# The head, the pair boundaries and the last norm of a two-block transformer kernel, put in another order

## The reference, cut to what matters

```python
def adaln(cond, w_ada, b_ada):                       # w_ada: 1024 x 3072
    m = jax.nn.silu(cond) @ w_ada + b_ada
    return jnp.split(m, 3, axis=-1)                  # shift, scale, gate

def hybrid_layer(...):
    shift, scale, gate = adaln(c, w_ada, b_ada)
    shift_c, scale_c, gate_c = adaln(c_ctx, w_ada, b_ada)
    h = rmsnorm(x, norm_g) * (1 + scale[:, None]) + shift[:, None]       # 1024 tokens
    hc = rmsnorm(ctx, norm_g) * (1 + scale_c) + shift_c                  # 256 tokens
    q, k, v, za, u, bg, cg, zc = jnp.split(h @ w_in, SPLIT_POINTS, axis=-1)
    q, k = rmsnorm(heads(q), q_norm_g), rmsnorm(heads(k), k_norm_g)
    kc, vc = jnp.split(hc @ w_in[:, D_ATTN:3 * D_ATTN], 2, axis=-1)
    attn = neighbourhood_attention(q, k, heads(v), kc, vc, rpb) * silu(za)
    conv = bg * centred_short_conv(cg * u, conv_w, conv_b) * silu(zc)
    x_new = x + gate[:, None] * (concat([attn, conv]) @ w_out)
...
    return _rmsnorm(x, g_final)                      # the end of the second block
```

## Time and profile before

| | us |
|---|---|
| three runs, median | 2747.57 |
| the three runs | 2745.29, 2747.57, 2747.58 |
| the profiled execution's own time | 2748.74 |
| its span | 2746.9 |
| PE busy | 2587.7 |
| DVE, ACT, POOL busy | 1107.1, 803.1, 765.7 |

### The profile page before, as it was taken

The page is one execution under the profiler, slowest core; times in us unless marked ns, Lnnn a source line. Parts: engine busy times, 40 slices in busy tenths (PEclk is TensorE's granted clock), DMA queues, the critical chain, the costliest instruction groups (busy, mean ns, idle before and its releaser), DMA issues.

```text
span 2746.9 us, 34507 instructions
## 1 busy us (share of the span) xinstructions
PE 2587.7 (94%) x12792; PEld 2128.9 (78%) x12792; DVE 1107.1 (40%) x1758; ACT 803.1 (29%) x1326; POOL 765.7 (28%) x492
## 2 busy tenths in 40 slices
PE   7899999999899999999999899997999999999997
PEld 2677877888787878778787688885788888888886
DVE  3553555545545544445444553444242121121123
ACT  3343444434412443344433521232021010010110
POOL 1131314122247222222222133323233333333331
PEclk9899999999999999999999999998999999999998
DMA  8412213030345222211222134210211111111111
GB/s 310 145 57 78 64 48 99 19 115 31 132 131 171 71 71 67 70 60 61 70 66 70 69 122 168 92 47 31 77 61 48 51 46 47 52 46 46 53 46 69
DMA packets 68165, 218.25 MB, mean 79 GB/s; under 512 B 21180, under 2 KB 21436, under 8 KB 63172
## 3 DMA queue, kind: packets, MB, share of 16 engines
q1 hardware_dynamic: 45316, 123.67, 14.2%
q10 hardware_dynamic: 22720, 92.81, 10.3%
HBM read 173.43 MB, written 35.16 MB: 76 GB/s over the span
## 4 chain that ended last, share of the span: by engine, by line
PE 74%; issue 7%; DVE 6%; ACT 5%; DMA 4%; POOL 1%; SPq 1%; ACTq 0%; DVEq 0%; POOLq 0%
PE ps L1869 14%; PE ps L1870 13%; PE ps L1872 13%; PE ps L1856 8%; PE ps L1857 8%; PE ps L1858 8%; DMA raw<-in_w_stream_dram 2%; PE ps L2262 1%; DMA ada<-in_w_ada_dram 1%; PE ps L2090 1%; PE ps L2066 1%; DVE stage L1679 1%; SPq L380 1%; ACT pt_hi L671 1%; ACT p_hi L968 1%
## 5 line engine op out<-in xcount | busy, mean ns | idle before, releaser
L410 POOL CAST w_hi<-raw 128x1024 fp32r<-128x1024 f32 x192 | 208.3, 1085 | 1753.1 <-issue 783.6
L1856 PE MATMUL ps<-act_hi,w_hi 128*128 128x512 f32 x1168 | 471.5, 404 | 12.3 <-POOL w_lo L412 9.0
L412 POOL TENSOR_TENSOR w_lo<-raw,w_hi 128x1024 fp32r<-128x1024 f32 x192 | 470.8, 2452 | 15.4
L1857 PE MATMUL ps<-act_lo,w_hi 128*128 128x512 f32 x1168 | 461.1, 395 | 5.6 <-issue 5.6
L1858 PE MATMUL ps<-act_hi,w_lo 128*128 128x512 f32 x1168 | 461.5, 395 | 0.0
L1869 PE MATMUL ps<-act_hi,w_hi 128*128 128x512 f32 x1008 | 396.4, 393 | 9.9 <-DVE act_lo L1208 5.3
L1870 PE MATMUL ps<-act_lo,w_hi 128*128 128x512 f32 x1008 | 394.8, 392 | 0.0
L1872 PE MATMUL ps<-act_hi,w_lo 128*128 128x512 f32 x1008 | 312.2, 391 | 0.0
L1856 PEld LDWEIGHTS ps<-act_hi,w_hi 128*128 128x128 f32 x1168 | 222.5, 190 | 53.2 <-POOL w_lo L412 9.2
L1858 PEld LDWEIGHTS ps<-act_hi,w_lo 128*128 128x128 f32 x1168 | 222.3, 190 | 49.3
L1857 PEld LDWEIGHTS ps<-act_lo,w_hi 128*128 128x128 f32 x1168 | 223.1, 191 | 45.5 <-issue 6.5
(11 more groups left out here) (360 smaller groups left out, 3926.2 us busy)
## 6 DMA issues: line engine op xcount, KB each, us to landing
raw<-in_w_stream_dram SPq DMA_DIRECT2D x192, 512.0 KB, 3.5
ada<-in_w_ada_dram SPq DMA_DIRECT2D x6, 2048.0 KB, 9.7
spill<-res ACTq DMA_DIRECT2D x16, 512.0 KB, 5.1
gate_dram<-gate_sb ACTq DMA_DIRECT2D x32, 256.0 KB, 2.0
stage<-spill ACTq DMA_DIRECT2D x16, 512.0 KB, 4.0
res<-in_x_t_dram ACTq DMA_DIRECT2D x1, 4096.0 KB, 19.3
rope_sb<-in_rope_dram ACTq DMA_DIRECT2D x4, 1024.0 KB, 4.9
stage<-in_x_t_dram ACTq DMA_DIRECT2D x8, 512.0 KB, 4.4
```

Source lines behind the costliest of these rows:

```text
L410: nc.gpsimd.tensor_copy(w_hi[:, s, :, :], raw[:, s, :, :]).then_inc(S["w_hi"], 1)
L412: nc.gpsimd.tensor_tensor(w_lo[:, s, :, :], raw[:, s, :, :], w_hi[:, s, :, :].bitcast(F), ALU.subtract).then_inc(S["w_split"], 1)
L1856: nc.tensor.matmul(out, wh, xh, start=start, stop=False)
L1857: nc.tensor.matmul(out, wh, xl, start=False, stop=False)
```

## The change

**Head.** The two halves of x are loaded first of all on ACT's queue. W_ada gets three buffers at the start; SP then loads block 3, tiles 0 and 1, ctx, blocks 4 and 5, tiles 2 and 3, and only then issues the Toeplitz transfers and the strip. In blocks 0 to 3 two of eight slices stay in plain fp32; the other six are split on the chip: ACT copies to fp32r (`ada_hi`, three copies of 128x1024 a block), DVE subtracts (`ada_lo`), and PE makes twelve fp32r matmuls with four columns of cond (high and low), whose rows are added after the transposes. Tiles 0 and 1 are projected together, slice by slice. The gate blocks come behind them as `gate_chunk`: W_ada is the stationary operand and one column of cond moves, so 32 products a block. The norm of ctx lies between and behind them, then the ctx keys.

**Pairs.** First half of Q's tile, ctx keys and second half of Q's tile move ahead of the pair's start, to the end of the pair before; the `hc` load moves to unit 14. Between `head_ss` and first spread stands the first half of V; the second half of V comes before `half_turn` of K, and only the ctx values are left between that and the second spread. Tile 4 is done in two halves, with the scores of units 0 and 1 and, behind the second, three convolution steps; ACT evacuates u after the first exponential. In the last pair convolution steps are kept for units 14 and 15, its mix is split in another order, and the first two W_out tiles take slices 0 to 3 before 4 to 7.

**End.** The last output tile is made in token halves, and square, sum, spread, scale and store follow half by half.

```diff
-                             w_stream[s].rearrange("p (k c) -> p k c", k=KT)
-                             ).then_inc(S[f"raw_in{s}"], 16)
+            def ada_load(n, used=0):
+                if used:
+                    sp.wait_ge(S["ada_used"], used)
+                sp.dma_start(ADA_SLOT[n], w_ada[n].rearrange("p (k c) -> p k c", k=KT)).then_inc(S[ADA_IN[n][0]], 16)
+
+            def tile_load(idx):
+                if idx >= 2:
+                    sp.wait_ge(S["w_split"], idx - 1)
+                sp.dma_start(raw[:, idx % 2, :, :], w_stream[idx].rearrange("p (k c) -> p k c", k=KT)
+                             ).then_inc(S[f"raw_in{idx % 2}"], 16)
+
+            ada_load(0)
+            ada_load(1)
+            ada_load(2)
+            ada_load(3, 1)
+            tile_load(0)
+            tile_load(1)
+            sp.dma_start(ctxF[:, :, :], ctx_t).then_inc(S["rows_in"], 16)
+            ada_load(4, 2)
+            ada_load(5, 3)
+            tile_load(2)
+            tile_load(3)
 
...
@@ -389,10 +410,12 @@
                                  w_stream[bass.ds(2 * h + s, 1)].rearrange("o p (k c) -> (o p) k c", k=KT)
                                  ).then_inc(S[f"raw_in{s}"], 16)
 
-            for k in range(KT):
...
@@ -421,7 +444,6 @@
             split(0, 0, free=False)
             split(0, 1, free=False)
 
-            pool.wait_ge(S["mask_in"], 16)
...
+                nc.scalar.activation(csq[:, k % 2, :], ctxF[:, k, :], ACT.Square).then_inc(S["sq_ready"], 1)
+
+            ada_hi(0)
+            for k in range(4):
+                x0_square(k)
+            ada_hi(1)
+            for k in range(4, 8):
+                x0_square(k)
+            ada_row(0)
+            ada_hi(2)
+            ada_row(1)
+            norm_rms("x0")
+            ada_hi(3)
+            ada_row(2)
+            ada_row(3)
             nc.scalar.activation(turn[:, :, :], traw[:, :].rearrange("p (a m) -> p a m", a=2), ACT.Copy)
-
-            act.wait_ge(S["ada_used"], 4)
-            nc.scalar.activation(mrow[:, 0:2 * D], ps[0:2, 0:4 * BANK], ACT.Copy).then_inc(S["ada_rows"], 1)
-            norm_rms("x0")
+            norm_hi("x0", {6: [lambda: ctx_square(0)], 7: [lambda: ctx_square(1)]})
+            for k in range(2, KT):
...
@@ -660,6 +712,8 @@
                     nc.scalar.activation(osh[here, :], na_o(m)[there, :], ACT.Copy).then_inc(S["na_osh"], 1)
 
                 exp_unit(0)
+                act.wait_ge(S["tile_done"], t0 + 5)
+                nc.scalar.activation(cv_x, ps[:, 4 * BANK:6 * BANK], ACT.Copy).then_inc(S["cv_u"], 1)
                 for u in range(16):
                     if u < 15:
                         exp_unit(u + 1)
@@ -673,7 +727,12 @@
                                          ).then_inc(S["na_pt_hi"], 1)
                     if u >= 2 and u % 2 == 0:
                         other_half(u // 2 - 1)
-                    for h in HALF_TAKEN.get(u, []):
+                    if u == 14 and not last_pair:
+                        act.wait_ge(S["na_scores"], 16 * i + 16)
+                        act.wait_ge(S["hc_saved"], 32)
+                        act.dma_start(hc_hi[:, :, :].bitcast(F), hc_dram[:, 0, :, :]).then_inc(S["hc_in"], 16)
+                        act.dma_start(hc_lo[:, :, :].bitcast(F), hc_dram[:, 1, :, :]).then_inc(S["hc_in"], 16)
...
+                if last_pair:
+                    act.wait_ge(S["tile_done"], T_OUT)
+                    mixed_hi(0)
...
+                    dve.wait_ge(S["hi_ready"], 4 * n + j + 1)
+                    nc.vector.tensor_tensor(act_lo[:, 3 * (n % 2) + j, :],
+                                            ADA_SLOT[n][:, 2 * j + 2:2 * j + 4, :].rearrange("p k c -> p (k c)"),
+                                            act_hi[:, 3 * (n % 2) + j, :].bitcast(F), ALU.subtract
+                                            ).then_inc(S["lo_ready"], 1 if j < 2 else 2)
+
+            ada_lo(0)
+            for k in range(4):
+                accumulate("x0", k, stage[:, k % 2, :])
+            ada_lo(1)
...
-            pe.wait_ge(S["c_silu"], 1)
-
             def ada_chunk(n):
-                pe.wait_ge(S[f"ada_in{n % 2}"], 16 * (n // 2) + 16)
-                for k in range(KT):
-                    last = nc.tensor.matmul(ps[0:2, (n % 4) * BANK:(n % 4 + 1) * BANK], cond[:, k, :],
-                                            ada[:, n % 2, k, :], start=(k == 0), stop=(k == KT - 1))
+
+                out = ps[0:4, n * BANK:(n + 1) * BANK]
+                pe.wait_ge(S[ADA_IN[n][0]], ADA_IN[n][1])
+                for k in range(2):
+                    nc.tensor.matmul(out, cond4[:, k, :], ADA_SLOT[n][:, k, :], start=(k == 0), stop=False)
+                for j in range(3):
+                    pe.wait_ge(S["lo_ready"], 4 * n + j + 1)
+                    for k in range(2):
+                        x = slice(k * BANK, (k + 1) * BANK)
+                        for part in (act_hi, act_lo):
+                            last = nc.tensor.matmul(out, cond4r[:, 2 * j + 2 + k, :], part[:, 3 * (n % 2) + j, x],
+                                                    start=False, stop=(j == 2 and k == 1 and part is act_lo))
                 last.then_inc(S["ada_used"], 1)
 
-            def turn_rows(m0, m1, b):
-
-                for m in range(m0, m1):
-                    last = nc.tensor.transpose(bank(b, 2 * m, 2 * m + 2), mrow[:, m * P:(m + 1) * P], ident[0:2, 0:2])
-                last.then_inc(S["ada_turned"], 1)
-
+            def gate_chunk(n):
+
+                pe.wait_ge(S[ADA_IN[n][0]], ADA_IN[n][1])
+                for m in range(4):
+                    for k in range(KT):
+                        c = 64 + 4 * (n - 4) + m
+                        last = nc.tensor.matmul(bank(4, c, c + 1), ADA_SLOT[n][:, k, m * P:(m + 1) * P],
+                                                cond4[:, k, 0:1], start=(k == 0), stop=(k == KT - 1))
+                return last
+
+            pe.wait_ge(S["c_sig"], 4)
             for n in range(4):
+                if n == 3:
+                    sum_squares("x0")
                 ada_chunk(n)
-            sum_squares("x0")
-            pe.wait_ge(S["ada_rows"], 1)
-            turn_rows(0, 16, 4)
+            spread("x0")
+            pe.wait_ge(S["ada_rows"], 4)
+            for m in range(16):
+                last = nc.tensor.transpose(bank(4, 4 * m, 4 * m + 4), mrow[:, m * P:(m + 1) * P], ident[0:4, 0:4])
+            last.then_inc(S["ada_turned"], 1)
+
+            tile_ready(T_ATT)
+            tile_ready(T_ATT + 1)
+            for k in range(KT):
+                for s in range(2):
+                    last = project(s, 2 * s, act_hi, act_lo, T, [k], filled("x0") if s == 0 else None, k == 0,
+                                   k == KT - 1)
+                    if k == KT - 1 and s == 0:
+                        last.then_inc(S["half_done"], 2)
+            gate_chunk(4)
             sum_squares("ctx")
-            spread("x0")
+            gate_chunk(5).then_inc(S["ada_turned"], 1)
             spread("ctx")
-            ada_chunk(4)
-            ada_chunk(5)
-            pe.wait_ge(S["ada_rows"], 2)
-            turn_rows(16, 24, 2)
-
-            tile_ready(T_ATT)
-            project(0, 0, act_hi, act_lo, T, ready=filled("x0")).then_inc(S["half_done"], 2)
+
+            def context_keys(i):
+                pe.wait_ge(S["hc_in"], 32 * i + 32)
+                return project(0, 6, hc_hi, hc_lo, C, ready=filled("ctx"))
+
+            context_keys(0).then_inc(S["tile_done"], 2)
+            pe.wait_ge(S["ada_step"], 5)
 
             def neighbourhood(i, last_pair):
...
@@ -1975,15 +2166,15 @@
                     last.then_inc(S["qk_perm"], 1)
 
                 head_ss(0, tD, 0)
-                project_half(1, 2, 1).then_inc(S["tile_done"], 1)
+                tile_ready(t0 + 2)
+                pe.wait_ge(S["pair_done"], i + 1)
+                project_half(0, 4, 0)
                 pe.wait_ge(S["ck_rms"], 2 * i + 1)
                 nc.tensor.matmul(bank(6, C, 2 * C), bd64, ksq, start=True, stop=True).then_inc(S["ck_ss"], 1)
                 head_spread(0, tD, 0)
-                tile_ready(t0 + 2)
-                project_half(0, 4, 0)
                 head_ss(1, tB, 2)
+                project_half(0, 4, 1)
                 half_turn(0, kh, 0)
-                project_half(0, 4, 1)
                 pe.wait_ge(S["conv_done"], i + 1)
...
@@ -2052,7 +2243,9 @@
 
                 scores(0)
                 scores(1)
-                done = 0
+                project_half(0, 4, 1).then_inc(S["tile_done"], 1)
+                conv_steps(0, 3)
+                done = 3
...
                         if u == 14:
@@ -2091,11 +2284,18 @@
                                                         start=(n == 0 and pt is pt_hi),
                                                         stop=(n == len(blocks) - 1 and pt is pt_lo))
                         last.then_inc(S["na_pv"], 1)
+                if not last_pair:
```

(28 more changed lines are left out.)

348 lines of the change are left out of this document (237 added, 111 removed).

## The result

The changed kernel took 2772.83 us, median of four runs (2770.34 to 2775.81), beside 2746.43 for the kernel before on the same chip: a ratio of 1.0096, 95% interval [1.0083, 1.011]. That is 26.4 us slower, where the forecast had 9.6 and a range that ended at 2770. The profiled execution spans 2770.6 us against 2746.9, so 23.7 us are there to be found in the trace.

The account below looks back on a forecast made before the run. PE's work plus its idle time was taken as the bound; +22.1 + 7.6 + 4.6 - 13.4 - 4.0 - 7.3 = +9.6 us on the profiled 2748.74 is 2758.3, forecast 2757 because that execution lies 1.2 above the median; range 2740 to 2770.

Parts of the forecast that it names:

- The sign: Whole kernel: the change makes it slower, +9.6 us in sum.
- the head: Start to second spread of pair 0: uncovered gate blocks and ctx behind x move that spread from 134.05 to 156.2, +22.1 us.
- The row at 52.12: Earlier profile's stretch granted 0.50 after PE's one- and two-column matmuls; taken as evidence that gate blocks fall to low clock.
- Last pair and W_out: Last pair's end: six steps for units 14 and 15 shrink waits, six thinner units open 0.3 each; -4.0 us.
- clock and exponential terms: Per pair: low clock behind the wait at the second spread costs 1.9 us, the earlier first exponential saves 3.35.
- Boundaries: Between pairs, last P times V to second spread: 42.4 us at jumps, 40.8 without; +1.8 plus issue stalls, +4.6 us.
- the stall: 2.8 us issue stall behind each of two jumps: full price or hidden in a wait, so half taken twice, +2.8 us.
- Low clock: Second spread, four times: PE waits 6.0 us for DVE, then runs at low clock, 1.9 us each, +7.6 us.
- First exponential: Start of units, four pairs: 2.1 us wait before first transposes and low clock behind it go; 3.35 each, -13.4 us.
- End: Behind PE's last product: half-wise norm and stores leave 18.2 us instead of 25.5, -7.3 us.
- stalls stay and the ramp is late: Rival: x scaled from 62 and both issue stalls in full with their low clock, +4 + 6, 2767 us; chance 0.14.

Follow-up runs that it names:

- aligned_last: Changed kernel with only the last pair's convolution steps dealt anew so each half of 8 ends with a unit; ratio 1.0064 to the kernel before.
- exp_late: Changed kernel with the start of the units put back in all pairs (u evacuated before the first exponential); ratio 1.0133 to the kernel before.
- tail_only: Kernel before with only the changed kernel's end (last tile, final norm and stores in halves); ratio 0.9968 to the kernel before.
- after_pad190: Changed kernel with 190 drains of PE ahead of its first product, so the pair loop covers 8 code stretches; ratio 1.0138 to the kernel before.
- row_gates: Changed kernel with gate blocks in the earlier row form, conditioning stationary and 512 columns moving, plus 176 drains; ratio 1.0057 to the kernel before.

## Why the forecast was wrong

The sign was right, and the head was: x scaled from 58.9 (forecast 58), joint projection to 87.5 (85.8), gate blocks 9.1 and 13.8 (11.4 and 14.3), second spread at 156.4 (156.2). The row at 52.12 was the right row for the clock. That the spread was hit to 0.2 us is partly luck: the projection ended 1.7 late, the gate blocks with ctx's sum and spread took some 3 less than forecast, and from the end of the first spread to the second it was 18.2 us where the earlier trace rows had 17.2.

**The step that failed is "Last pair and W_out", -4.0.** It said that units 14 and 15 get six steps and that six thinner units "open 0.3 each". I read the number of steps in a unit and not where a half of eight ends. In the list of the kernel before the halves end exactly with units 1, 4, 6, 9, 11 and 13; in the new list of the last pair, with the three steps ahead counted, five of them end inside units 2, 5, 7, 10 and 13, and the next step waits for bank 7 to be read by DVE while the rest of PE's program stands behind it. With the clock and exponential terms of that pair I had -5.4; it was +8.0, and that miss of 13.4 is nearly the whole distance between +9.6 and +23.7. The other misses, +3.0, -4.0, +3.5 and -2.1, are not small, and cancel by luck. aligned_last shows the cause by taking it away: over the same stretch its trace is 10.5 us shorter (135.3 for 145.8). The last 2.9 of the 13.4 stay unexplained.

**Boundaries, +4.6, were +0.6.** The 42.4 us without stall was 41.4, with a wait of 7.26 where I had 6.0: DVE's order is the same, but its low part of K (L1394) took 2.21 us where it took 1.22 in the kernel before (L1274); why is open. For the stall I took half twice, +2.8, and none came. The Trainium skill (Runtime: NRT & Kernel Launch, Instruction fetch mechanics) has 16 KiB blocks, and a fetch behind a taken jump whose target is outside a window of two blocks. The size of a block agrees with the trace. The fetch does not: this loop, of 7 blocks by count, was gone through again without one. The earlier trace rows I read twice too simply. The same view has a second part of each of the two stalls, which I left out, so that each is some 4.5 us and not 2.8:
```profile
PE ps L1856 <- issue: 3.3, 2, 1.8
```
And I took it at its word: "issue" ended the wait last, but just behind it stood a late load and ACT's evacuation. So the issue stall was worth nothing in the kernel before and would be worth some 5 us in the changed one, where it does not occur.

**Low clock, +7.6:** right; in pair 3 the spread takes 1.97 us where it took 1.09, and the half tile behind it 6.7 where it took 5.7. **First exponential, -13.4:** the wait went, and the term was too large: 6.9 in three pairs by the trace of exp_late, 10.2 in four by its ratio. Of the 3 us that the units of pairs 0 to 2 fell short all lie in pair 2; pairs 0 and 1 came out 1.5 and 1.4 shorter, as forecast. In pair 2 the profiled execution of the kernel before had no low clock behind the old wait (112.60 us at 1.00; tail_only, with the same pairs, has 114.24 at 0.99), and the changed one had more of it behind the spread (0.50 from 460.91 to 471.15). The first is the chance of that execution.

**End, -7.3:** mis-sized, 8.8 alone and 9.4 in the changed kernel's trace. Three half scales of half 0 ran ahead of half 1's reciprocal and five behind it, while PE spread half 1; DVE did its last 13 half scales in one piece of 8.62 us. Behind the last product 18.2 us were forecast and 15.2 came.

**Not in the forecast: +3.5** between W_out and the last MLP. In the memory attention's loop, which by count covers 8 stretches in both kernels, the changed one has stalls behind its jumps, which the kernel before has not; PE's waits, 1090 to 1280 us:
```profile
PE ps L2029 <- issue: 2.7, 2, 1.5
```
These are 2.7 of the 3.5. Before, that loop was fetched anew as well and did not stall. By count it begins 94 instructions into a stretch there and 13 into one here. Whether that decides was not tried.

The rival "stalls stay and the ramp is late" had the nearest number, 2767, and neither of its causes.

## What to carry to other kernels

When work is dealt out in steps between other work, check where each accumulation ends, not only how many steps a slot has: a group that ends inside a slot makes its successor wait for its own evacuation at once. A wait's releaser is only the last of those that were late; take it away and look before pricing it, and take suspects away both singly and together, for here one alone gave nothing, the other alone 10.7 us, and the two 17.3. Before moving a half tile to fill one wait, see which wait it is covering now: here 7.26 us of waiting for DVE came into the open, and putting two small DVE operations ahead took 5 of them away.

## What the runs showed of the hardware

- A loop of 1680 PE instructions (804 matmuls and 804 weight loads of a turn are in the trace) that by count covered 7 stretches of 256 in the code was not fetched again in its second and third turn, one of the same length that covered 8 was: 0 or 1 packet of code against 15 to 17 between 270 and 560 us, in three kernels each. Inserting 32 drains ahead of it was enough to change from one to the other.
- With fetches back in the loop, PE stalled 1.8 and 2.5 us behind the two jumps in after_pad190, and the boundaries grew by 4.6 and 5.2: over half of the price is PE's longer busy time at the low clock behind it.
- fp32 products of one column, each with a 128x128 weight load, were granted 1.2 GHz from 92.27 us on, though PE had not paused since 62.8 and worked on to 112.0. In row_gates, with 512 moving columns, a block took 7.03 us at a granted 1.00, instead of 9.12 and 13.79.
